# Stick-breaking attention beside a short convolution: units head by head, loads a head ahead, transposes before scores

## The chip, the cores and the metric

The kernel runs on one core of a Trainium2 chip. The metric is the device time of one execution in microseconds (us). Engines: TensorE (PE; its weight loads PEld), VectorE (DVE), ScalarE (ACT), GpSimd (POOL) and SyncE (SP), which issues the DMAs.

## The reference

One decoder layer on x of 2048 tokens by 1024, in float32. h = RMSNorm(x); one projection gives q, k, v (8 heads of 64) and B, C, u (512 columns each). q and k are normed per head. Then, side by side:

- stick-breaking attention, strictly causal: with z = q.k / 8, A[t,s] = sigmoid(z[t,s]) times the product over s < j < t of (1 - sigmoid(z[t,j])), out = A v;
- a gated convolution: y = B * conv3(C * u), causal, width 3, per channel.

Both are put side by side, multiplied by w_out and added to x; then RMSNorm and a SwiGLU FFN of width 2816, added to x.

## The kernel before, in words

Stages follow each other with all engines in step between them: qkv_stage (norm, q, k, v, written to DRAM), attend_conv_stage (the change is in it alone), and for each half of the tokens mix_stage and ffn_stage. Operands of matmuls are split into a high and a low part (fp32r), so most products are three matmuls (matmul3, L70 to L72).

attend_conv_stage goes over four **pairs** of heads. For a pair, and a head h, the 2048 queries are 8 groups g of 256 (two tiles t of 128). The keys up to a tile are cut into **units** of at most 8 blocks of 128 keys, from the last keys to the first: tiles 0 to 7 have one unit of t + 1 blocks, tiles 8 to 15 one of t - 7 blocks and one of 8. That is 24 units a head and 48 a pair, with 272 blocks. Before the change groups rise and the two heads take turns, group by group.

A unit n passes through the engines so:

- TensorE, scores(n): two matmuls of up to 512 columns per bank (L881, L882) and, on the diagonal, a mask (L885) into z, which has two banks' pairs: scores(n) wait until scan n-2 is done;
- ScalarE, sigmoids(n): sigmoid(z) to a (L675) and sigmoid(-z) back into z (L677);
- VectorE, running_product(n): a scan over the unit (L760) into stick;
- GpSimd, a_unit(n): a times stick (L821);
- TensorE, transposes(n) (L897), LAG = 3 slots later: four blocks make a **fill** of tr, which has two fills; a fill waits until VectorE is done with the fill two before it;
- ScalarE copies a fill to aT_hi (L688), VectorE subtracts it to aT_lo (L772);
- TensorE, a_times_v(gi) once all units of a group are through (L912), then o_low (ScalarE, L695) and o_sb (VectorE, L781), and a store.

Every engine runs a list of **slots**, one for each unit, in program order. In slot n VectorE does scan(n), then aT_lo(n-3); ScalarE does sigmoids(n), then aT_hi(n-3); TensorE does scores(n), half of the slot's projection steps, transposes(n-3), the other half, and at a group's end a_times_v.

Between them TensorE computes the projection of B, C and u for 512 tokens a pair: 12 outputs (NPROJ) of 8 steps of 3 matmuls into one bank, proj. A planner (own, weight, ratio) spreads the 96 steps over the slots by the columns that a slot has of its own. Before the change ScalarE copies C out of proj (L719), VectorE multiplies u (L787) and B (L799) straight from proj, GpSimd convolves (L837 to L842). ScalarE and GpSimd split the weights (w_split, L711 and L847).

SyncE issues the loads. At the start of a pair it issues q, w, k, all 8 parts of hT and v; k and v of a pair can go only when the units that read the old ones are through.

## Time and profile before

| | |
|---|---|
| median of 3 runs | 2892.89 us (2890.64 to 5896.87) |
| profiled execution | 2895.9 us, its span 2894.1 us |
| TensorE busy | 2675.9 us, 92% of the span |
| VectorE busy | 1447.6 us, 50% |
| ScalarE busy | 907.9 us, 31% |
| GpSimd busy | 557.3 us, 19% |
| DMA | 246.33 MB, mean 85 GB/s |
| mean granted TensorE clock | 0.967 of 2.4 GHz |

Times are from the start of the span. An instruction's line is that of the kernel; L70 to L72 are the helper for three matmuls. Matmuls are pipelined: one shown with 0.39 us is followed by the next after 0.23 us, so a busy TensorE is not one at its peak, and spacing is read from starts. The attention stage takes some 850 us of the span, the FFN most of the rest.

### The profile page before, as it was taken

Reading aid. Unit: us, or ns where it says so; the run is one execution under the profiler, and the core shown is the slowest. Engines: PE = TensorE matmul, PEld = TensorE weight load, DVE = VectorE, ACT = ScalarE, POOL = GpSimd, SP = SyncE. Lnnn points to the kernel's source line nnn. Section 1 sums busy time; section 2 is a strip of 40 time slices with the busy share of each in tenths; the row PEclk is TensorE's granted clock in tenths of the full one; section 3 lists DMA queues with packets and bytes.
Section 4 is the critical chain, followed back from the end, with each engine's and each line's share of the span. In section 5 each row is a group of like instructions: output and inputs, shape, how many; then the busy total and the mean of one; then the engine's idle time right before and its main releaser. Section 6 shows DMA issues by size and latency. Waiting matters only on the chain. (4 is left out here: it accounts for less than half of the span.)

```text
span 2894.1 us, 36348 instructions
## 1 busy us (share of the span) xinstructions
PE 2675.9 (92%) x12800; PEld 2205.3 (76%) x12800; DVE 1447.6 (50%) x1536; ACT 907.9 (31%) x1423; POOL 557.3 (19%) x426
## 2 busy tenths in 40 slices
PE   6999679799898898799999999999789999999998
PEld 5888567677677677587888888887678888888887
DVE  4333256566576577443454444444434444544444
ACT  3222256566566566322111111111221111111110
POOL 1222146556466466100000000000000000000000
PEclk9999889899899999899999999999899999999999
DMA  5555652531631630412111111100621111111101
GB/s 173 176 172 169 173 150 60 137 109 52 167 85 54 173 84 25 154 50 88 44 56 45 43 51 43 58 29 8 225 73 59 44 51 43 55 47 43 51 29 58
DMA packets 301153, 246.33 MB, mean 85 GB/s; under 512 B 14193, under 2 KB 272241, under 8 KB 300273
## 3 DMA queue, kind: packets, MB, share of 16 engines
q1 hardware_dynamic: 301040, 244.90, 28.3%
q8 instruction: 63, 1.03, 0.1%
q14 instruction: 50, 0.40, 0.1%
HBM read 186.13 MB, written 58.72 MB: 85 GB/s over the span
## 5 line engine op out<-in xcount | busy, mean ns | idle before, releaser
L1281 DVE TENSOR_TENSOR all_acc<-all_acc,ffn_down 128x1024 f32<-128x1024 f32 x352 | 426.0, 1220 | 374.3 <-PE ffn_down L72 356.9
L760 DVE TENSOR_TENSOR_SCAN att_stick<-att_z,att_stick 128x128 f32<-128x128 f32 (+3 forms) x192 | 331.0, 1724 | 269.5 <-ACT att_z L677 268.4
L821 POOL TENSOR_TENSOR att_a<-att_a,att_stick 128x128 f32<-128x128 f32 (+3 forms) x192 | 281.6, 1471 | 338.1 <-DVE att_stick L760 324.6
L70 PE MATMUL ffn_gate<-all_h2T_hi,ffn_gu_hi 128*128 128x512 f32 x704 | 276.6, 393 | 8.2 <-DVE ffn_gu_lo L1271 8.2
L70 PE MATMUL ffn_down<-ffn_d_hi,ffn_hid_hi 128*128 128x512 f32 x704 | 277.0, 393 | 6.2 <-DVE ffn_hid_lo L1303 6.1
L71 PE MATMUL ffn_down<-ffn_d_lo,ffn_hid_hi 128*128 128x512 f32 x704 | 276.1, 392 | 0.0
L71 PE MATMUL ffn_gate<-all_h2T_lo,ffn_gu_hi 128*128 128x512 f32 x704 | 276.0, 392 | 0.0
L72 PE MATMUL ffn_down<-ffn_d_hi,ffn_hid_lo 128*128 128x512 f32 x704 | 276.0, 392 | 0.0
L72 PE MATMUL ffn_gate<-all_h2T_hi,ffn_gu_lo 128*128 128x512 f32 x704 | 275.8, 392 | 0.0
L70 PE MATMUL ffn_up<-all_h2T_hi,ffn_gu_hi 128*128 128x512 f32 x704 | 273.9, 389 | 0.0
L71 PE MATMUL ffn_up<-all_h2T_lo,ffn_gu_hi 128*128 128x512 f32 x704 | 273.9, 389 | 0.0
L72 PE MATMUL ffn_up<-all_h2T_hi,ffn_gu_lo 128*128 128x512 f32 x704 | 273.9, 389 | 0.0
L1292 DVE TENSOR_TENSOR ffn_hid<-ffn_silu,ffn_up 128x512 f32<-128x512 f32 x88 | 60.6, 688 | 400.4 <-PE ffn_up L72 400.4
L1261 ACT ACTIVATE ffn_hid_hi<-ffn_hid 128x512 fp32r<-128x512 f32 x88 | 55.7, 632 | 605.8 <-DVE ffn_hid L1292 605.8
L897 PE MATMUL att_tr<-all_ident,att_a 128*128 128x128 f32 x1088 | 170.9, 289 | 74.6 <-DVE att_aT_lo L772 74.3
L1252 ACT ACTIVATE ffn_silu<-ffn_gate 128x512 f32<-128x512 f32 x88 | 52.7, 598 | 582.0 <-PE ffn_gate L72 582.0
L675 ACT ACTIVATE att_a<-att_z 128x128 f32<-128x128 f32 (+3 forms) x192 | 149.2, 777 | 227.1 <-PE att_z L885 157.1
L897 PEld LDWEIGHTS att_tr<-all_ident,att_a 128*128 128x128 f32 x1088 | 131.0, 147 | 115.3 <-DVE att_aT_lo L772 80.6
L70 PE MATMUL att_proj<-att_hT_hi,att_w_hi 128*128 128x512 f32 x384 | 175.4, 457 | 28.8 <-DMA att_hT_lo<-hT_lo 11.6
L772 DVE TENSOR_TENSOR att_aT_lo<-att_tr,att_aT_hi 128x512 fp32r<-128x512 f32 (+2 forms) x320 | 180.4, 594 | 28.2 <-ACT att_aT_hi L688 19.0
L1042 POOL TENSOR_TENSOR mix_msq<-mix_ss,all_eps 128x1 f32<-128x1 f32 x16 | 3.0, 190 | 965.4 <-ACT mix_square L1075 965.4
L688 ACT ACTIVATE att_aT_hi<-att_tr 128x512 fp32r<-128x512 f32 (+2 forms) x320 | 159.2, 531 | 71.6 <-PE att_tr L897 70.9
(108 smaller groups left out, 5222.2 us busy)
## 6 DMA issues: line engine op xcount, KB each, us to landing
att_w_stage<-in_w_in SPq DMA_DIRECT2D x48, 512.0 KB, 4.4
ffn_d_stage<-in_w_down SPq DMA_DIRECT2D x44, 512.0 KB, 3.4
all_stage<-in_w_gate SPq DMA_DIRECT2D x22, 512.0 KB, 3.8
all_stage<-in_w_up SPq DMA_DIRECT2D x22, 512.0 KB, 4.7
ffn_gu_stage<-in_w_gate SPq DMA_DIRECT2D x22, 512.0 KB, 3.7
ffn_gu_stage<-in_w_up SPq DMA_DIRECT2D x22, 512.0 KB, 4.7
qkv_x_t<-in_x SPq DMA_DIRECT2D x16, 512.0 KB, 4.5
hT_hi<-qkv_hT_hi SPq DMA_DIRECT2D x16, 512.0 KB, 5.4
```

Of the source, the lines that this page charges most:

```text
L70: nc.tensor.matmul(out, lhs_hi, rhs_hi, start=first, stop=False)
L71: nc.tensor.matmul(out, lhs_hi, rhs_lo, start=False, stop=False)
L72: return nc.tensor.matmul(out, lhs_lo, rhs_hi, start=False, stop=last)
L675: nc.scalar.activation(a[:, n % 4, 0:nb * P], z[:, n % 2, 0:nb * P], ACT.Sigmoid, scale=SCALE).then_inc(chance_done, 1)
L688: nc.scalar.activation(aT_hi[:, gi % 2, j0 + j:j0 + j + nj, (t % GT) * P:(t % GT + 1) * P], tr[:, f % 2, 0:nj, :], ACT.Copy).then_inc(aT_h ...
L760: nc.vector.tensor_tensor_scan(stick[:, row % 2, c0:c1][:, ::-1], z[:, n % 2, 0:nb * P][:, ::-1], stick[:, row % 2, S:S + 1].to_broadcast( ...
L772: nc.vector.tensor_tensor(aT_lo[:, gi % 2, blocks, toks], tr[:, f % 2, 0:nj, :], aT_hi[:, gi % 2, blocks, toks].bitcast(F32), ALU.subtract ...
L821: nc.gpsimd.tensor_tensor(a[:, n % 4, 0:nb * P], a[:, n % 4, 0:nb * P], stick[:, row_of[n] % 2, c0:c0 + nb * P], ALU.mult).then_inc(a_done, 1)
L897: last = nc.tensor.transpose(tr[:, f % 2, i, :], a[:, n % 4, (j + i) * P:(j + i + 1) * P], cst["ident"][:, :])
L1261: nc.scalar.activation(hid_hi[:, b, n * BANK:(n + 1) * BANK], hid[:, n % 2, :], ACT.Copy).then_inc(hid_hi_done, 1)
L1281: nc.vector.tensor_tensor(acc[:, t, :], acc[:, t, :], down[:, t % 2, :, :].rearrange("p h n -> p (h n)"), ALU.add).then_inc(acc_done, 1)
L1292: nc.vector.tensor_tensor(hid[:, n % 2, :], silu[:, n % 2, :], up[:, n % 2, :], ALU.mult).then_inc(hid_done, 1)
```

## The change

Four things:

1. **Order of units.** All groups of head 0, then all of head 1; in a head the groups go 4, 3, 5, 2, 6, 1, 7, 0.
2. **Loads.** q lies in a ring of four groups and is loaded two groups ahead, k and v a head ahead, hT and the first weights of a pair at the end of the pair before.
3. **The projection's results** are all copied out of proj by ScalarE (take), GpSimd multiplies C*u and B*conv. TensorE waits for one semaphore, proj_out.
4. **TensorE's slot**: transposes(n-3), then scores(n), then all projection steps, then a_times_v. The planner's costs are new.

VectorE's list keeps scan(n) ahead of aT_lo(n-3), ScalarE's keeps sigmoids(n) ahead of aT_hi(n-3). The first and the last pair are written out, the two between are a loop. The diff, cut:

```diff
@@ -441,7 +434,9 @@
     KB = S // P
     GW = 2 * P
     GT = GW // P
-    NG = 2 * (S // GW)
+    HG = S // GW
+    NG = 2 * HG
+    QB = 4
     SLOT = 2 * BANK
     SB = SLOT // P
     LAG = 3
@@ -451,30 +446,34 @@
     NPROJ = 3 * CT
     HALO = TAPS - 1
     COL0 = w_in.shape[1] - 3 * CD
-    assert S // BANK == PAIRS
-
-
-    units, opens = [], []
-    for gi in range(NG):
+    assert S // BANK == PAIRS and NG % QB == 0
+
+    rising = [g for g in range(HG // 2, HG)]
+    falling = [HG - 1 - g for g in rising]
+    groups = [(h, g) for h in range(2) for pair in zip(rising, falling) for g in pair]
+    units, opens, row_of, row_end = [], [], [], []
+    for gi, (h, g) in enumerate(groups):
         for i in range(GT):
-            t = GT * (gi // 2) + i
+            t = GT * g + i
             for j0 in reversed(range(0, t + 1, SB)):
                 opens.append(not units or units[-1][0] != gi)
-                units.append((gi, gi % 2, t, j0, min(SB, t + 1 - j0)))
-    NU = len(units)
+                units.append((gi, h, t, j0, min(SB, t + 1 - j0)))
+                row_of.append(len(row_end))
+            row_end.append(len(units))
+    NU, ROWS = len(units), len(row_end)
     fills = [0]
     for u in units:
         fills.append(fills[-1] + -(-u[4] // 4))
     FILLS = fills[-1]
-    assert NU % 4 == 0 and FILLS % 2 == 0
+    assert NU % 4 == 0 and FILLS % 2 == 0 and ROWS % 2 == 0
     group_units = [sum(u[0] < gi for u in units) for gi in range(NG + 1)]
-    head_end = [max(n for n, u in enumerate(units) if u[1] == h) + 1 for h in range(2)]
-
-
+    head_end = [group_units[HG], NU]
 
     FIRST, LAST = 1, NU - 1
-    own = [u[4] + (GT * (units[n - LAG][0] // 2 + 1) if n > LAG and opens[n - LAG] else 0)
-           for n, u in enumerate(units)]
+    own = []
+    for n, u in enumerate(units):
+        av = 2.1 * (groups[units[n - LAG - 1][0]][1] + 1) if opens[n - LAG] else 0
+        own.append(0.5 * u[4] + 0.45 * units[n - LAG][4] + av)
     weight = [u[4] + 1.7 for u in units]
     ratio = (sum(own[FIRST:LAST]) + 3 * NPROJ * KT) / sum(weight[FIRST:LAST])
     steps, placed, goal, spent = [[] for _ in units], 0, 0.0, 0.0
@@ -491,16 +489,13 @@
     starts = {n: k for n in range(NU) for k, i in steps[n] if i == 0}
     ends = {n: k for n in range(NU) for k, i in steps[n] if i == KT - 1}
     assert len(starts) == len(ends) == NPROJ
-
-
-    row_of, row_end = [], []
-    for n, (gi, h, t, j0, nb) in enumerate(units):
-        if j0 + nb == t + 1:
-            row_end.append(n)
-        row_of.append(len(row_end) - 1)
-        row_end[-1] = n + 1
-    ROWS = len(row_end)
-    assert ROWS % 2 == 0
+    emptied = {n + 1: k for n, k in ends.items()}
+    taken = {k: n for n, k in emptied.items()}
+    multiplied = {taken[3 * c + 1]: c for c in range(CT)}
+    tapped_at = {taken[3 * c + 1] + 1 + d: (c, d) for c in range(CT) for d in range(2)}
@@ -547,38 +549,40 @@
         tr_full, aT_hi_done, aT_lo_done = m.sem("tr_full"), m.sem("aT_hi_done"), m.sem("aT_lo_done")
         o_full, o_low_done, o_done = m.sem("o_full"), m.sem("o_low_done"), m.sem("o_done")
         o_stored = [m.sem("o_stored0"), m.sem("o_stored1")]
-        w_hi_done, w_lo_done, proj_full = m.sem("w_hi_done"), m.sem("w_lo_done"), m.sem("proj_full")
-        c_done, cu_done, conv_chain, conv_done, y_done, y_stored = (
-            m.sem(n) for n in ("c_done", "cu_done", "conv_chain", "conv_done", "y_done", "y_stored"))
+        w_hi_done, w_lo_done, proj_full, proj_out = (
+            m.sem(n) for n in ("w_hi_done", "w_lo_done", "proj_full", "proj_out"))
+        cu_done, conv_chain, conv_done, y_done, y_stored = (
+            m.sem(n) for n in ("cu_done", "conv_chain", "conv_done", "y_done", "y_stored"))
         block = m.block()
 
         def pairs(eng, body):
             body(0)
-            with eng.Fori(1, PAIRS) as p:
+            with eng.Fori(1, PAIRS - 1) as p:
                 body(p)
...
-            def load_k(p, h, keys, loaded):
-                wait(sp, z_full, NU * p + head_end[h] - NU)
+            def load_k(p, h):
+                wait(sp, z_full, NU * (p - 1) + head_end[h])
                 rows = bass.ds((2 * p + h) * HD + AD, HD)
                 for half, src in enumerate((qk_hi_dram, qk_lo_dram)):
-                    sp.dma_start(k_st[half * HD:(half + 1) * HD, h, keys].bitcast(F32),
-                                 src[rows, keys]).then_inc(loaded, DMA)
+                    sp.dma_start(k_st[half * HD:(half + 1) * HD, h, :].bitcast(F32),
+                                 src[rows, :]).then_inc(k_in[h], DMA)
 
             def load_q(p, gi):
-                h, g = gi % 2, gi // 2
-                q, gq = at(p, gi - 4, NG)
+                h, g = groups[gi]
+                q, gq = at(p, gi - QB, NG)
                 wait(sp, z_full, q * NU + group_units[gq + 1])
-                rows = bass.ds((2 * p + h) * HD, HD)
+                rows = bass.ds((2 * p + h) * HD, HD) if g else bass.ds(p * P + h * HD, HD)
                 for half in range(2):
                     part = slice(half * HD, (half + 1) * HD)
                     for dst, src in ((q_hh, qk_hi_dram), (q_ll, qk_lo_dram)):
-                        sp.dma_start(dst[part, h, g % 2, :].bitcast(F32),
-                                     src[rows, g * GW:(g + 1) * GW]).then_inc(q_in[h][g % 2], DMA)
+                        sp.dma_start(dst[part, gi % QB, :].bitcast(F32),
+                                     src[rows, g * GW:(g + 1) * GW]).then_inc(q_in[gi % QB], DMA)
 
             def load_v(p, h):
-                wait(sp, o_full, NG * p + h - 1)
+                wait(sp, o_full, NG * (p - 1) + HG * (h + 1))
                 sp.dma_start(v_st[:, h, :, :].bitcast(F32), v_dram.rearrange("(j p) h d -> p j h d", p=P)
                              [:, :, bass.ds(2 * p + h, 1), :].rearrange("p j h d -> p j (h d)")).then_inc(v_in[h], DMA)
 
...
+            def start_up():
+                load_k(0, 0)
+                load_q(0, 0)
+                load_w(0, 0)
+                for i in range(KT // 2):
+                    load_hT(0, i)
+                load_w(0, 1)
+                load_q(0, 1)
+                for i in range(KT // 2, KT):
+                    load_hT(0, i)
+                load_v(0, 0)
+                with nc.allow_non_contiguous_dma(reason="conv weights, once"):
+                    for c in range(CT):
+                        sp.dma_start(taps[:, c, :], conv_w[:, c * P:(c + 1) * P].rearrange("w p -> p w")
+                                     ).then_inc(taps_in, DMA)
+
+            def body(p):
+                if is_first(p):
+                    start_up()
+                for n, (gi, h, t, j0, nb) in enumerate(units):
+                    if opens[n]:
+                        if gi + 2 < NG:
+                            load_q(p, gi + 2)
+                        elif not is_last(p):
+                            load_q(p + 1, gi + 2 - NG)
+                        if gi >= 3 or not is_first(p):
+                            store_o(p, gi - 3)
+                    if n == 2:
+                        load_k(p, 1)
+                        if not is_first(p):
+                            store_y(p - 1, CT - 1)
+                    if n == LAG + 3:
+                        load_v(p, 1)
+                    if n in starts and starts[n] + 2 < NPROJ:
+                        load_w(p, starts[n] + 2)
+                    if n - 2 in gated and gated[n - 2] < CT - 1:
+                        store_y(p, gated[n - 2])
+                    if not is_last(p):
+                        if n == head_end[0] + 2:
+                            load_k(p + 1, 0)
+                        if n == head_end[0] + LAG + 3:
+                            load_v(p + 1, 0)
+                        for i in reloads.get(n, ()):
+                            load_hT(p + 1, i)
+                        if n == taken[NPROJ - 1]:
+                            load_w(p + 1, 0)
+                            load_w(p + 1, 1)
 
...
-                wait(act, halo_moved, 2 * (CT * p + c))
-                if isinstance(p, int) and c == 0:
-                    act.wait_ge(edges_set, 2)
-                nc.scalar.activation(cu[:, 0:HALO], halo[:, c, :], ACT.Copy).then_inc(halo_moved, 1)
-
-            def keep_halo(p, c):
-                act.wait_ge(cu_done, CT * p + c + 1)
-                nc.scalar.activation(halo[:, c, :], cu[:, BANK:BANK + HALO], ACT.Copy).then_inc(halo_moved, 1)
+            def take(p, k):
+                c = k // 3
+                if k % 3 == 1:
+                    wait(act, conv_done, CT * p + c)
+                    wait(act, halo_moved, 2 * (CT * p + c))
+                    if is_first(p) and c == 0:
+                        act.wait_ge(edges_set, 2)
+                    nc.scalar.activation(cu[:, 0:HALO], halo[:, c, :], ACT.Copy).then_inc(halo_moved, 1)
+                act.wait_ge(proj_full, NPROJ * p + k + 1)
+                if k % 3 == 0:
+                    wait(act, cu_done, CT * p + c)
+                    nc.scalar.activation(c_sb[:, :], proj[:, :], ACT.Copy).then_inc(proj_out, 1)
+                elif k % 3 == 1:
+                    nc.scalar.activation(cu[:, HALO:HALO + BANK], proj[:, :], ACT.Copy).then_inc(proj_out, 1)
+                else:
+                    wait(act, y_stored, DMA * (CT * p + c))
+                    nc.scalar.activation(y[:, :], proj[:, :], ACT.Copy).then_inc(proj_out, 1)
+                    act.wait_ge(cu_done, CT * p + c + 1)
+                    nc.scalar.activation(halo[:, c, :], cu[:, BANK:BANK + HALO], ACT.Copy).then_inc(halo_moved, 1)
 
             def w_split(p, k):
                 act.wait_ge(w_in_sem[k % 2], (DMA * NPROJ // 2) * p + DMA * (k // 2 + 1))
...
             def body(p):
+                if is_first(p):
+                    w_split(p, 0)
                 for n in range(NU):
-                    if ends.get(n - 1, 1) % 3 == 0:
-                        c = ends[n - 1] // 3
-                        act.wait_ge(proj_full, NPROJ * p + ends[n - 1] + 1)
-                        wait(act, cu_done, CT * p + c)
-                        nc.scalar.activation(c_sb[:, :], proj[:, :], ACT.Copy).then_inc(c_done, 1)
-                        set_halo(p, c)
+                    if n in emptied:
+                        take(p, emptied[n])
+                    q, b = at(p, n - LAG - 1)
+                    if opens[b] and (n - LAG - 1 > 0 or not is_first(p)):
+                        o_part(q, units[b][0] - 1)
                     sigmoids(p, n)
-                    if ends.get(n - 1, 0) % 3 == 1:
-                        keep_halo(p, ends[n - 1] // 3)
-                    if n >= LAG or not isinstance(p, int):
+                    if n >= LAG or not is_first(p):
                         aT_part(p, n - LAG)
-
-                    q, b = at(p, n - LAG - 1)
-                    if opens[b] and (n - LAG - 1 > 0 or not isinstance(p, int)):
-                        o_part(q, units[b][0] - 1)
-                    if n == 0:
-                        w_split(p, 0)
                     if n in starts and starts[n] + 1 < NPROJ:
                         w_split(p, starts[n] + 1)
+                    if n == taken[NPROJ - 1] and not is_last(p):
+                        w_split(p + 1, 0)
 
@@ -821,6 +816,11 @@
                 nc.gpsimd.tensor_tensor(a[:, n % 4, 0:nb * P], a[:, n % 4, 0:nb * P],
                                         stick[:, row_of[n] % 2, c0:c0 + nb * P], ALU.mult).then_inc(a_done, 1)
 
+            def c_times_u(p, c):
+                pool.wait_ge(proj_out, NPROJ * p + 3 * c + 2)
+                nc.gpsimd.tensor_tensor(cu[:, HALO:HALO + BANK], cu[:, HALO:HALO + BANK], c_sb[:, :],
+                                        ALU.mult).then_inc(cu_done, 1)
+
             CHAIN = 2 * TAPS - 2
 
             def convolve(p, c, part):
@@ -842,22 +842,33 @@
                 nc.gpsimd.tensor_tensor(conv[:, :], conv[:, :], tapped[:, :],
                                         ALU.add).then_inc(conv_done if part == TAPS - 1 else conv_chain, 1)
 
+            def gate(p, c):
+                pool.wait_ge(proj_out, NPROJ * p + 3 * c + 3)
+                pool.wait_ge(conv_done, CT * p + c + 1)
+                nc.gpsimd.tensor_tensor(y[:, :], y[:, :], conv[:, :], ALU.mult).then_inc(y_done, 1)
+
...
+                    w_split(p, 0)
                 for n in range(NU):
-                    for part in range(TAPS):
-                        k = ends.get(n - 1 - part, 0)
-                        if k % 3 == 1:
-                            convolve(p, k // 3, part)
+                    if n in multiplied:
+                        c_times_u(p, multiplied[n])
+                    if n in tapped_at:
+                        c, d = tapped_at[n]
+                        for part in ((0, 1), (2,))[d]:
+                            convolve(p, c, part)
+                    if n in gated:
+                        gate(p, gated[n])
                     a_unit(p, n)
-                    if n == 0:
-                        w_split(p, 0)
                     if n in starts and starts[n] + 1 < NPROJ:
                         w_split(p, starts[n] + 1)
+                    if n == taken[NPROJ - 1] and not is_last(p):
+                        w_split(p + 1, 0)
 
             pairs(pool, body)
 
...
-                        wait(pe, y_done, CT * p + k // 3)
-                    elif k % 3 == 1:
-                        pe.wait_ge(c_done, CT * p + k // 3 + 1)
-                    else:
-                        pe.wait_ge(cu_done, CT * p + k // 3 + 1)
+                    wait(pe, proj_out, NPROJ * p + k)
                 last = matmul3(nc, proj[:, :], w_hi[:, k % 2, i, :], w_lo[:, k % 2, i, :],
                                hT_hi[:, i, :], hT_lo[:, i, :], i == 0, i == KT - 1)
                 if i == KT - 1:
@@ -935,17 +937,13 @@
 
             def body(p):
                 for n in range(NU):
+                    if n >= LAG or not is_first(p):
+                        transposes(p, n - LAG)
                     scores(p, n)
-
-                    early = 0 if n in starts else (len(steps[n]) + 1) // 2
-                    for k, i in steps[n][:early]:
-                        project_step(p, k, i)
-                    if n >= LAG or not isinstance(p, int):
-                        transposes(p, n - LAG)
-                    for k, i in steps[n][early:]:
+                    for k, i in steps[n]:
                         project_step(p, k, i)
                     q, b = at(p, n - LAG)
-                    if opens[b] and (n > LAG or not isinstance(p, int)):
+                    if opens[b] and (n > LAG or not is_first(p)):
                         a_times_v(q, units[b][0] - 1)
 
             pairs(pe, body)
...
```

## Rows read from the trace of the kernel before

**Rows 1.** The attention stage by pair: stretch and length in us, busy us (instructions) by engine.

```profile
342.60:561.00 218.40, 176.38 (x984) 144.44 (x985) 125.69 (x142) 122.88 (x208) 118.34 (x79) 0.91 0.45 118
561.00:768.20 207.20, 180.21 (x1043) 148.69 (x1042) 136.48 (x155) 126.88 (x216) 121.81 (x81) 0.95 0.40 109
...
971.70:1164.50 192.80, 171.82 (x997) 142.17 (x998) 127.13 (x146) 124.08 (x212) 114.27 (x76) 0.97 0.27 72
```

**Rows 2.** TensorE in order of time: start us, us, then the merged instructions.

```profile
376.20 0.39 PE L70 MATMUL att_proj<-att_hT_hi,att_w_hi 128*128 128x512 f32 x1
376.42 0.39 PE L71 MATMUL att_proj<-att_hT_lo,att_w_hi 128*128 128x512 f32 x1
...
558.38 0.28 PE L912 MATMUL att_o<-att_aT_lo,att_v_st 128*128 128x256 f32 x1
558.50 0.28 PE L912 MATMUL att_o<-att_aT_hi,att_v_st 128*128 128x256 f32 x1
...
706.70 0.82 PE L897 MATMUL att_tr<-all_ident,att_a 128*128 128x128 f32 x6
```

**Rows 3.** Waits in the whole kernel, and what the projection's engines waited for.

```profile
PE att_tr L897 <- DVE att_aT_lo L772: 74.3, 69, 4.3
...
  DMA att_hT_lo<-hT_lo: 29.1, 7
...
  DMA att_w_stage<-in_w_in: 18.9, 3
```

**Rows 4.** An 8-block unit from its scores to the next transposes, all engines.

```profile
705.08 0.39 PE L881 MATMUL att_z<-att_k_st,att_q_hh 128*128 128x512 f32 x1
...
706.20 1.03 ACT L675 ACTIVATE att_a<-att_z 128x1024 f32<-128x1024 f32 x1 [0.57 <-PE att_z L882]
...
707.13 1.02 ACT L677 ACTIVATE att_z<-att_z 128x1024 f32<-128x1024 f32 x1
...
708.18 2.35 DVE L760 TENSOR_TENSOR_SCAN att_stick<-att_z,att_stick 128x1024 f32<-128x1024 f32 x1 [1.27 <-ACT att_z L677]
...
710.45 0.99 DVE L772 TENSOR_TENSOR att_aT_lo<-att_tr,att_aT_hi 128x512 fp32r<-128x512 f32 x2
...
711.17 1.16 PE L897 MATMUL att_tr<-all_ident,att_a 128*128 128x128 f32 x8 [2.18 <-DVE att_aT_lo L772]
```

**Rows 5.** A 5-block unit, all engines.

```profile
701.57 0.44 PE L881 MATMUL att_z<-att_k_st,att_q_hh 128*128 128x512 f32 x1
...
703.86 1.55 DVE L760 TENSOR_TENSOR_SCAN att_stick<-att_z,att_stick 128x640 f32<-128x640 f32 x1 [0.27 <-ACT att_z L677]
...
705.33 1.26 DVE L772 TENSOR_TENSOR att_aT_lo<-att_tr,att_aT_hi 128x512 fp32r<-128x512 f32 x2
```

**Rows 6.** Granted clock (PEclk) of three stretches, and eight transposes at either level.

```profile
566.00:576.00 10.00, 6.72 (x20) 5.01 (x21) 3.32 (x6) 4.14 (x9) 5.27 (x3) 0.50 0.88 197
870.00:890.00 20.00, 18.49 (x119) 15.70 (x118) 12.92 (x13) 13.88 (x22) 9.96 (x6) 1.00 0.31 83
1173.00:1182.00 9.00, 5.82 (x24) 4.55 (x24) 5.31 (x10) 3.96 (x7) 2.00 (x1) 0.50 0.03 7
...
563.88 1.12 PE L897 MATMUL att_tr<-all_ident,att_a 128*128 128x128 f32 x8 [2.43 <-DVE att_aT_lo L772]
...
566.04 1.97 PE L897 MATMUL att_tr<-all_ident,att_a 128*128 128x128 f32 x8 [0.73 <-DVE att_aT_lo L772]
```

**Rows 7.** Reads of proj and what follows: count, busy us, mean ns, idle before.

```profile
L842 POOL TENSOR_TENSOR att_conv<-att_conv,att_tapped 128x512 f32<-128x512 f32 x32 | 41.1, 1285 | 2.5
...
L799 DVE TENSOR_TENSOR att_y<-att_proj,att_conv 128x512 f32<-128x512 f32 x16 | 11.0, 686 | 14.8 <-POOL att_conv L842 11.3 <-issue 3.4
...
L719 ACT ACTIVATE att_c_sb<-att_proj 128x512 f32<-128x512 f32 x16 | 9.6, 599 | 2.7 <-PE att_proj L72 2.6
```

**Rows 8.** The busiest stretch of the DMA engines at a joint.

```profile
550.00:570.00 20.00, 14.60 (x92) 12.26 (x92) 11.95 (x15) 11.23 (x19) 13.19 (x10) 0.88 0.98 272
```

**Rows 9.** The last instruction of the stage on VectorE.

```profile
1188.58 0.42 DVE L781 TENSOR_TENSOR att_o_sb<-att_o,att_o_low 64x256 f32<-64x256 f32 x1 [6.36 <-ACT att_o_low L695]
```

More of the change, by code:

```diff
@@ L493, in attend_conv_stage @@
     assert len(starts) == len(ends) == NPROJ
-    row_of, row_end = [], []
-    for n, (gi, h, t, j0, nb) in enumerate(units):
-        if j0 + nb == t + 1:
-            row_end.append(n)
-        row_of.append(len(row_end) - 1)
-        row_end[-1] = n + 1
-    ROWS = len(row_end)
-    assert ROWS % 2 == 0
+    emptied = {n + 1: k for n, k in ends.items()}
+    taken = {k: n for n, k in emptied.items()}
+    multiplied = {taken[3 * c + 1]: c for c in range(CT)}
+    tapped_at = {taken[3 * c + 1] + 1 + d: (c, d) for c in range(CT) for d in range(2)}
+    gated = {taken[3 * c + 2]: c for c in range(CT)}
+    assert all(taken[3 * c + 2] >= taken[3 * c + 1] + 2 for c in range(CT)) and max(taken.values()) < NU
+    reloads = {n + 1: [i for k, i in steps[n] if k == NPROJ - 1] for n in range(NU)}
     def key_slot(n):
@@ L512, in at, with is_first, is_last @@
         return (p, n) if n >= 0 else (p - 1, n + per)
+    def is_first(p):
+        return isinstance(p, int) and p == 0
+    def is_last(p):
+        return isinstance(p, int) and p == PAIRS - 1
     with ExitStack() as stack:
@@ L537, in attend_conv_stage @@
         proj = m.ps("proj", [P, BANK])
-        k_first = [m.sem("k_first0"), m.sem("k_first1")]
         k_in, v_in = [m.sem("k_in0"), m.sem("k_in1")], [m.sem("v_in0"), m.sem("v_in1")]
-        q_in = [[m.sem(f"q_in{h}{b}") for b in range(2)] for h in range(2)]
+        q_in = [m.sem(f"q_in{b}") for b in range(QB)]
         hT_in = [m.sem(f"hT_in{i}") for i in range(KT)]
@@ L602, in store_o @@
                 p, gi = at(p, gi, NG)
[L603 removed]
+                h, g = groups[gi]
                 sp.wait_ge(o_done, NG * p + gi + 1)
[L605 removed]
+                rows = bass.ds((2 * p + h) * HD, HD) if g else bass.ds(2 * (p * HD) + h * HD, HD)
+                sp.dma_start(mixT_dram[rows, g * GW:(g + 1) * GW],
                              o_sb[:, gi % 2, :]).then_inc(o_stored[gi % 2], DMA)
[L608 to L653 removed]
@@ L753, in running_product @@
                 if j0 + nb == t + 1:
-                    if row >= 2 or not isinstance(p, int):
+                    if row >= 2 or not is_first(p):
                         q, r = at(p, row - 2, ROWS)
@@ L781, in o_part @@
                 nc.vector.tensor_tensor(o_sb[:, gi % 2, :], o[0:HD, 0:GW], o_low[:, :], ALU.add).then_inc(o_done, 1)
-            def c_times_u(p, c):
-                dve.wait_ge(halo_moved, 2 * (CT * p + c) + 1)
-                dve.wait_ge(c_done, CT * p + c + 1)
-                dve.wait_ge(proj_full, NPROJ * p + 3 * c + 2)
-                nc.vector.tensor_tensor(cu[:, HALO:HALO + BANK], proj[:, :], c_sb[:, :], ALU.mult).then_inc(cu_done, 1)
             def body(p):
                 for n in range(NU):
-                    k = ends.get(n - 1, 0)
-                    if k % 3 == 1:
-                        c_times_u(p, k // 3)
-                    if k % 3 == 2:
-                        c = k // 3
-                        dve.wait_ge(proj_full, NPROJ * p + k + 1)
-                        dve.wait_ge(conv_done, CT * p + c + 1)
-                        wait(dve, y_stored, DMA * CT * p + DMA * c)
-                        nc.vector.tensor_tensor(y[:, :], proj[:, :], conv[:, :], ALU.mult).then_inc(y_done, 1)
                     running_product(p, n)
-                    if n >= LAG or not isinstance(p, int):
+                    if n >= LAG or not is_first(p):
                         aT_part(p, n - LAG)
                     q, b = at(p, n - LAG - 1)
-                    if opens[b] and (n - LAG - 1 > 0 or not isinstance(p, int)):
+                    if opens[b] and (n - LAG - 1 > 0 or not is_first(p)):
                         o_part(q, units[b][0] - 1)
@@ L830, in convolve @@
                 if part == 0:
-                    if isinstance(p, int) and c == 0:
+                    if is_first(p) and c == 0:
                         pool.wait_ge(taps_in, DMA * CT)
@@ L867, in scores @@
                 gi, h, t, j0, nb = units[n]
[L868 removed]
                 if opens[n]:
[L870 to L872 removed]
+                    if gi % HG == 0:
                         pe.wait_ge(k_in[h], 2 * DMA * p + 2 * DMA)
[L874 removed]
+                    pe.wait_ge(q_in[gi % QB], 4 * DMA * (NG // QB) * p + 4 * DMA * (gi // QB + 1))
                 wait(pe, scan_done, NU * p + n - 1)
@@ L880, in scores @@
                     out, keys = z[:, n % 2, b0:b1], slice(j0 * P + b0, j0 * P + b1)
-                    nc.tensor.matmul(out, q_hh[:, h, g % 2, tile], k_st[:, h, keys], start=True, stop=False)
-                    last = nc.tensor.matmul(out, q_ll[:, h, g % 2, tile], k_st[:, h, keys],
+                    nc.tensor.matmul(out, q_hh[:, gi % QB, tile], k_st[:, h, keys], start=True, stop=False)
+                    last = nc.tensor.matmul(out, q_ll[:, gi % QB, tile], k_st[:, h, keys],
                                             start=False, stop=not diagonal)
```

67 lines of the change are left out of this document (6 added, 61 removed).

## The prediction

> **What bounds the kernel now.** Everything that the change touches lies in the attention stage, whose four head pairs begin at 342.6, 561.0, 768.2 and 971.7 us; the last result of the stage is written at 1189.0 [rows 1, 9]. TensorE is busy for 0.81 to 0.89 of each pair, VectorE for 0.58 to 0.66, ScalarE and GpSimd for less, so TensorE's own work comes first. How much of it is work and not pipelining: a 512-column matmul follows the last one after 0.23 us at full clock, a 256-column one after 0.12 us (0.117 as the mean of a long run of them), and six transposes take 0.82 us with a tail of some 0.2 us, so 0.105 to 0.11 us each [rows 2]. A pair has 96 projection steps of 3 matmuls (288 x 0.23 = 66 us), 272 key blocks of scores (each 2 x 0.057 = 31 us) and 32 masks (3 us), 272 transposes (29 us) and 288 products with v (32 us): 161 us. A pair takes 193 to 218 us. The rest is in the waits: ahead of the transposes TensorE waits 74.3 us in all for VectorE's aT_lo, the one large wait it has; and at the joints of the pairs it waits for loads (29.1 us for hT; ScalarE 18.9 us for w) [rows 3]. So TensorE comes close to being the bound, because its waits are short, and they are short for a reason that the change takes away.
>
> **The reason.** VectorE's list for slot n is scan(n), then aT_lo(n-3). The transposes of slot n need the tr banks that aT_lo(n-4) frees, and that stands behind scan(n-1). Today scores(n) come ahead of this wait: they need only scan(n-2). So the loop from scores to scores over TensorE, ScalarE and VectorE closes once in **two** slots. The trace shows it: the scan that starts at 703.86 runs to 705.41, and the next unit's scores start at 705.08, before its end [rows 4, 5].
>
> **Part 1, the order inside a slot: the loop closes in one slot.** After the change scores(n+1) stand behind the transposes of unit n-2, these behind aT_lo(n-3), this behind scan(n), this behind both sigmoids of n, and these behind scores(n). Nothing in the chain can start early; z's two banks no longer help. Its price is in the trace. For a unit of 8 blocks [rows 4]: scores start 705.08, first sigmoid 706.20 (a), second 707.13 (z), scan 708.18, aT_lo 710.45, next transposes 711.17: 6.09 us. For one of 5 blocks [rows 5]: scores 701.57, scan 703.86, aT_lo 705.33, and with 0.67 us for it and 0.05 to the next engine 706.05: 4.48 us. From both: 1.79 us + 0.537 us per block.
> The new order of a pair has 48 units and 272 blocks. The wait is there where unit n-2 or n-3 has over 4 blocks (two fills of tr). That fails six times a pair (slots 1, 2, 19, 25, 26, 43, 36 blocks together), where TensorE's own work decides: I count 20 us for the six. The other 42 slots have 236 blocks: 42 x 1.79 + 236 x 0.537 = 202 us. To it comes what stands between the wait and the scores: the transposes of the last fill, 130 in the 42 slots x 0.11 = 14 us; and where both units have two fills (22 slots), the second aT_lo, some 0.45 us = 10 us. Sum 202 + 14 + 10 + 20 = **246 us a pair**, against 193 to 218. TensorE's 161 us fit under it: projection and products with v come behind the scores and run while the chain is on the other engines; only the six free slots are counted by TensorE's work.
> Bounds: below, the hops could be shorter (both samples are ones in which each link started when the one before ended), 5% or 12 us a pair less; above, ScalarE's added work may get into the chain (part 3), 5% more.
>
> **Part 2, TensorE's clock.** In the new order TensorE works 161 of 246 us, with a lull in nearly every slot: in 21 of 48 slots the chain is 2.0 to 3.4 us longer than the work. In the dense stretch at 870 us the granted clock is 1.00 (the 2.4 GHz level), at 566 to 576 us, behind waits of 2.43 us and 0.73 us, it is 0.50 (1.2 GHz), and in 1173 to 1182 us, the stage's drain, where TensorE does nothing but 24 transposes with waits between, also 0.50 [rows 6]. At the low level the same eight transposes take 1.97 instead of 1.12 us [rows 6], and the scores double too (0.93 us more for 8 blocks). Work at the low level fills the lulls, so after a slot or so the clock comes back, as it did in that joint. I count ten to twelve falls a pair at about 1 us each: 12 us a pair. Bounds: 0; and at most the low clock for half of the time, 24 us for scores, masks and last transposes (31 + 3 + 14 = 48 at full clock), with the lost cover some 35 us.
> The Trainium skill (TensorE: Matmul & The Clock Gate, Part 4, PE-mode transpose) says that transposes don't count as work for the clock. By that rule the lulls would be wider, and the term nearer to 35 us a pair (+140 us in all). The sum goes by the 12 us above, since the rows don't tell transposes from idling.
>
> **Part 3, what moves to ScalarE and GpSimd.** The c, C*u and y reads of proj go to ScalarE (32 more copies of 0.60 us = 19 us in the stage), the two products to GpSimd (32 of 1.3 us at most = 41 us), 32 of 0.69 us leave VectorE (22 us) [rows 7]. ScalarE does its copies before sigmoids(n), while TensorE stands at the transposes; GpSimd works 114 to 122 us of a pair [rows 1] and has three slots for each a. I count nothing. Cover gone, it is 19 us at most.
>
> **Part 4, the loads.** k, v and q come a head ahead, so the joints' waits end. One new wait: ScalarE's w_split for the next pair stands behind unit 46, its w load behind 4 MB of hT that are issued from slot 44 on. The DMAs moved 272 GB/s at their best [rows 8], so 4.5 MB need 17 us, and from the start of slot 44 to that place are 16 us less some 2 us until the first load. I count 4 us, three times: 12 us; behind that ScalarE wait stand sigmoids(47), and all of the chain. Bounds 0 and 10 us each. At the start the first scores need a whole k (1 MB) and not a quarter: 2 us; then hT as before, some 5 us of waiting beside a chain of 8-block units.
>
> **Part 5, the ends.** The drain from the last scores (about 1164.5, where the fourth stretch of [rows 1] is cut) to 1189.0 [rows 9] is three 8-block units and 32 products; now the last units have 1 and 2 blocks: 3 us.
>
> **The sum.** Start 345 + 5, four pairs 984, clock 48, w 12, drain 3: the stage ends at 1397 against 1189, **+208 us**. The profiled execution took 2895.9 us (span 2894.1), 3 us over the median of the runs shown: 2896 + 208 = 3104.
>
> **The rivals.**
> - *Balance wins (faster).* If the transposes don't wait for scan(n), because aT_lo is ahead often enough, the gain is the joints: a pair falls to TensorE's 161 us plus its dense stretches' slack (0.92 busy at 870 us [rows 6]), 175 us; 4 x 175 + 353 = 1053, so 136 us less: 2760 us. It decides if aT_lo(n-3) could go before scan(n); the listing of VectorE has it behind. Chance 0.03.
> - *The waits cancel.* If only half of the slots are gated (say, where fills are shared in another way than I read), a pair takes 205 us and the time stays: 2890 us. Chance 0.03.
> - *The clock stays low.* If the lulls keep the clock at 0.50 for the whole stage, TensorE's 161 us become 322 and the bound, 350 + 4 x 322 + 10 = 1648: +459, 3355 us. For it speaks the drain, which stayed at 0.50; against it, that at the low level TensorE is busy without lulls, and behind such work the clock came back at the joint. Chance 0.05. The Trainium skill (the same page, "HAM oscillation") describes kernels whose every burst starts slow after a wait; by that rule this case is the one to expect.
>
> **How the numbers follow.** The forecast has 0.89: slower by about 7%. Low end: chain 5% shorter (-49), no fall of the clock (-48), no wait for w (-12): 2995; not all at once, 3020. High end: chain 5% longer, clock at its upper bound for part (+60): 3210. What a measurement of this kernel can't tell from no change is about 2%, 58 us: all of the forecast's range is past it. Faster 0.03, same 0.03, slower 0.94.
>
> **What would show it.** The wait of TensorE's transposes for aT_lo grows from 74 us to some 300 us; scores start right behind the transposes, and scan(n) starts 3.1 us behind the scores of an 8-block unit in every slot; scan starts of neighbouring 8-block slots 6 to 7 us apart; pairs of 246 to 270 us, all four nearly alike; granted clock between 0.75 and 0.95 in the stage; the FFN as before. Wrong it would be if VectorE showed aT_lo(n-3) done while scan(n) still ran, if pairs took under 215 us, or if ScalarE's copies stood between transposes and sigmoids.

## The result, and the profile after

The changed kernel takes 3148.19 us (median of 4 runs, 3140.77 to 3156.74) against 2892.22: ratio 1.089, 95% interval 1.085 to 1.092. It is slower by 256 us, where 208 was forecast. Its profiled execution took 3156.74 us, its span is 3155.0 us.

The page: busy us by engine, then TensorE's busy tenths and its granted clock in 40 slices. TensorE's share falls from 92% to 87%, and the slices of the attention stage (the 5th to the 18th) show it at 5 to 7 tenths and at 0.7 to 0.9 of the clock, without the peaks and dips of before.

```profile
PE 2753.5 (87%) x12800; PEld 2261.8 (72%) x12800; DVE 1430.5 (45%) x1504; ACT 913.3 (29%) x1455; POOL 595.4 (19%) x458
...
PE   6999577677767767776899999999978999999999
...
PEclk9999788898988989988999999999989999999999
```

The four pairs of the changed kernel, from first scores to first scores (the fourth to its last scores), columns as in [rows 1]: 266 to 282 us each against 193 to 218, granted clock 0.84 to 0.90 against 0.91 to 0.97. VectorE is 17 us less busy in the whole kernel than before (1430.5 against 1447.6) and ScalarE 5 us more (913.3 against 907.9), so neither accounts for the time.

```profile
344.20:626.30 282.10, 203.12 (x1002) 164.88 (x1002) 126.50 (x138) 128.34 (x220) 132.22 (x89) 0.84 0.36 98
626.30:896.30 270.00, 198.48 (x1043) 161.89 (x1041) 129.16 (x144) 128.37 (x224) 130.11 (x88) 0.87 0.29 78
896.30:1168.60 272.30, 196.60 (x1043) 160.94 (x1041) 129.06 (x144) 128.25 (x224) 129.95 (x88) 0.88 0.29 78
1168.60:1434.40 265.80, 195.30 (x1031) 159.44 (x1030) 127.03 (x141) 125.66 (x219) 126.97 (x86) 0.90 0.18 47
```

Behind the stage the time is the same: from its last VectorE instruction to the end of the span are 1705 us in both kernels (3155.0 - 1450.0, and 2894.1 - 1189.0). So all of the time is in the attention stage.

The waits of its engines: us in total, number of waits, the longest. TensorE's transposes wait 294.2 us for aT_lo, against 74.3 [rows 3], and VectorE's scan 582 us for the sigmoids.

```profile
DVE att_stick L770 <- ACT att_z L683: 582.2, 190, 12.4
...
PE att_tr L905 <- DVE att_aT_lo L782: 294.2, 151, 8.7
...
ACT att_w_hi L726 <- DMA att_w_stage<-in_w_in: 47.1, 6, 16.1
```

One 8-block slot of the changed kernel, from its scores to the next (slot 45 of the second pair), answers to [rows 4]. Read it downwards: each row starts when the one above ends, or within 0.1 us of it (the transposes when the first of the two aT_lo is through), and the scores at 881.75 come right behind the transposes. Of what the next scores need, only ScalarE's copy to aT_hi, which isn't among the rows, runs beside another link, the scan. 7.05 us for one unit. Before, the scores at 705.08 started while the scan of the unit ahead still ran [rows 4, 5].

```profile
874.70 0.48 PE L889 MATMUL att_z<-att_k_st,att_q_hh 128*128 128x512 f32 x1
...
875.91 1.03 ACT L681 ACTIVATE att_a<-att_z 128x1024 f32<-128x1024 f32 x1 [4.02 <-PE att_z L890]
...
876.84 1.02 ACT L683 ACTIVATE att_z<-att_z 128x1024 f32<-128x1024 f32 x1
...
877.89 2.35 DVE L770 TENSOR_TENSOR_SCAN att_stick<-att_z,att_stick 128x1024 f32<-128x1024 f32 x1 [3.22 <-ACT att_z L683]
...
880.16 1.13 DVE L782 TENSOR_TENSOR att_aT_lo<-att_tr,att_aT_hi 128x512 fp32r<-128x512 f32 x2
...
880.88 1.12 PE L905 MATMUL att_tr<-all_ident,att_a 128*128 128x128 f32 x8 [2.05 <-DVE att_aT_lo L782]
...
881.75 0.31 PE L889 MATMUL att_z<-att_k_st,att_q_hh 128*128 128x128 f32 x1
```

And the joint between the second and the third pair on ScalarE: it stands at the weights for 7.75 us, and sigmoids of slot 47 (892.59) behind it.

```profile
882.80 1.07 ACT L694 ACTIVATE att_aT_hi<-att_tr 128x512 fp32r<-128x512 f32 x2
891.63 1.06 ACT L726 ACTIVATE att_w_hi<-att_w_stage 128x1024 fp32r<-128x1024 f32 x1 [7.75 <-DMA att_w_stage<-in_w_in]
892.59 0.37 ACT L681 ACTIVATE att_a<-att_z 128x256 f32<-128x256 f32 x1
```

### The profile page after: what moved, and what is told of

It is laid out like the page before. It is cut to its first block and busy times, and to the rows that moved or that the text cites. A ratio compares the mean times of both kernels' runs of the same rounds, so it can differ in the third digit from the quotient of the medians.

```text
span 3155.0 us, 35761 instructions
## 1 busy us (share of the span) xinstructions
PE 2753.5 (87%) x12800; PEld 2261.8 (72%) x12800; DVE 1430.5 (45%) x1504; ACT 913.3 (29%) x1455; POOL 595.4 (19%) x458
## 5 line engine op out<-in xcount | busy, mean ns | idle before, releaser
L770 DVE TENSOR_TENSOR_SCAN att_stick<-att_z,att_stick 128x128 f32<-128x128 f32 (+5 forms) x192 | 331.5, 1727 | 588.2 <-ACT att_z L683 582.2
L905 PE MATMUL att_tr<-all_ident,att_a 128*128 128x128 f32 x1088 | 193.9, 316 | 296.3 <-DVE att_aT_lo L782 294.2
L905 PEld LDWEIGHTS att_tr<-all_ident,att_a 128*128 128x128 f32 x1088 | 138.5, 158 | 353.0 <-DVE att_aT_lo L782 198.2
L816 POOL TENSOR_TENSOR att_a<-att_a,att_stick 128x128 f32<-128x128 f32 (+5 forms) x192 | 282.3, 1471 | 535.2 <-DVE att_stick L770 535.1
L681 ACT ACTIVATE att_a<-att_z 128x128 f32<-128x128 f32 (+5 forms) x192 | 149.1, 777 | 500.5 <-PE att_z L893 344.1
L889 PE MATMUL att_z<-att_k_st,att_q_hh 128*128 128x512 f32 (+2 forms) x320 | 150.6, 470 | 18.8 <-DMA att_q_ll<-qk_lo 15.4
```

The lines of the kernel that those rows point to most:

```text
L681: nc.scalar.activation(a[:, n % 4, 0:nb * P], z[:, n % 2, 0:nb * P], ACT.Sigmoid, scale=SCALE).then_inc(chance_done, 1)
L770: nc.vector.tensor_tensor_scan(stick[:, row % 2, c0:c1][:, ::-1], z[:, n % 2, 0:nb * P][:, ::-1], stick[:, row % 2, S:S + 1].to_broadcast( ...
L816: nc.gpsimd.tensor_tensor(a[:, n % 4, 0:nb * P], a[:, n % 4, 0:nb * P], stick[:, row_of[n] % 2, c0:c0 + nb * P], ALU.mult).then_inc(a_done, 1)
L889: nc.tensor.matmul(out, q_hh[:, gi % QB, tile], k_st[:, h, keys], start=True, stop=False)
L905: last = nc.tensor.transpose(tr[:, f % 2, i, :], a[:, n % 4, (j + i) * P:(j + i + 1) * P], cst["ident"][:, :])
```

## The experiments

Eleven kernels, in three sets; every ratio is to the kernel before on the same chip. A difference in us between two runs can cross chips; the kernel before took 2890.96 to 2892.22 us on all of them.

**1. e_swap: scores first again, the rest of the rewrite kept.**

```
-transposes(p, n - LAG); scores(p, n)
+scores(p, n); transposes(p, n - LAG)
```

> The changed kernel with one thing undone: in TensorE's slot the scores of n come ahead of the transposes of n-3 again; the projection steps stay behind both. Theory (the loop scores, sigmoids, scan, aT_lo, transposes closes in one slot): with scores first it closes in two slots, TensorE's own 161 us a pair and its waits decide again, a pair takes 190 to 210 us, the kernel 2830 to 2900 us. Rival (the other parts of the rewrite cost the time: unit order, copies on ScalarE, loads): pairs stay near 270 us, the kernel above 3080 us.

Measured: 2879.71 us, ratio 0.997 (0.995 to 0.998). Pairs of 201 to 210 us (the third is below), the wait for aT_lo in the whole kernel 113.0 us, longest 13.1.

```profile
756.90:958.00 201.10, 175.22 (x1039) 147.20 (x1040) 128.53 (x144) 130.69 (x224) 129.75 (x88) 0.96 0.37 97
```

```profile
PE att_tr L905 <- DVE att_aT_lo L782: 113.0, 88, 13.1
```

One pair of lines swapped on one engine is worth 268 us. The rest of the rewrite costs nothing and gains 12 us as it stands.

**2. e_half: TensorE's list of before.**

```
-transposes; scores; all steps
+scores; half of the steps; transposes; the other half
```

> The changed kernel with TensorE's list of before: scores, half of the projection steps, transposes, the other half. Theory: as with scores first alone, and the wait for aT_lo is covered by projection steps, so 5 to 20 us a pair less than it: pairs of 180 to 195 us, the kernel 2780 to 2860 us. Rival (the rest of the rewrite costs the time): above 3080 us.

Measured: 2869.27 us, ratio 0.992 (0.991 to 0.994). The cover by projection steps is worth 10 us, 2.6 a pair: less than expected. Pairs take 198 to 206 us, above the 180 to 195 expected; the kernel is 9 us outside the range. Run 7 shows a part of what hid the gain: the joint.

**3. e_oldtr: the old kernel with the new order of TensorE alone.**

```
-scores; half of the steps; transposes; the other half
+transposes; scores; all steps
```

> The kernel before with one part of the change alone: TensorE does the transposes, then the scores, then all projection steps. Theory: the loop closes in every slot, its sum over the same 48 units is again about 246 us a pair, to which the joints and the clock come: pairs of 255 to 280 us, the kernel 3110 to 3200 us. Rival (the order inside the slot matters little): 2880 to 2950 us.

Measured: 3159.21 us, ratio 1.093 (1.091 to 1.094). The second pair, and the wait:

```profile
641.90:908.20 266.30, 196.38 (x1043) 159.02 (x1042) 133.85 (x152) 124.93 (x216) 121.55 (x81) 0.90 0.29 80
```

```profile
PE att_tr L897 <- DVE att_aT_lo L772: 283.7, 148, 4.4
```

In another order of units, with other loads and with proj read by VectorE, the new order on TensorE costs 267 us. This is the whole effect of the change, and 11 us over. (The edit also puts all projection steps behind the scores; by runs 1 and 2 that part is worth some 10 us.) The first pair took 300.2 us, outside of the 255 to 280 expected; why wasn't looked into. The others took 264 to 270.

**4. e_aT: transposes still first, but the other two lists turned as well.**

```
 # ScalarE
-sigmoids(p, n); aT_part(p, n - LAG)
+aT_part(p, n - LAG); sigmoids(p, n)
 # VectorE
-running_product(p, n); aT_part(p, n - LAG)
+aT_part(p, n - LAG); running_product(p, n)
```

> The changed kernel, TensorE's list as changed (transposes first), but ScalarE does aT_hi of n-3 ahead of the sigmoids of n and VectorE aT_lo of n-3 ahead of scan n. Theory: then the transposes of the next slot need an aT_lo that stands ahead of scan n and not behind it; the loop opens to two slots though TensorE's order is untouched, and the kernel takes 2800 to 2920 us. Rival (transposes ahead of scores cost by themselves, by delaying the scores on TensorE): near 3150 us.

Measured: 2840.18 us, ratio 0.983 (0.981 to 0.985). TensorE's list is that of the change, transposes ahead of scores, and the wait for aT_lo is down to 66.1 us:

```profile
PE att_tr L905 <- DVE att_aT_lo L782: 66.1, 28, 13.3
```

So it is not the transposes' own time ahead of the scores that costs. What costs is that aT_lo stands behind a scan that stands behind the scores. The rival falls. ScalarE's and VectorE's lists were turned together in every run that has this edit; what either does alone wasn't run.

**5. e_wload: the next pair's weights ahead of its hT.**

```
-load_hT(p + 1, i) ...; load_w(p + 1, 0); load_w(p + 1, 1)
+load_w(p + 1, 0); load_w(p + 1, 1); load_hT(p + 1, i) ...
```

> The changed kernel, the two weight loads of the next pair issued ahead of the next pair's hT loads and not behind them. Theory: ScalarE's wait for w at the three joints (7.75 us at one of them) goes, the last slot of a pair takes 4.5 instead of 10.1 to 11.2 us: 15 to 30 us less, 3120 to 3135 us. Rival (the wait is hidden, or hT comes later by as much and TensorE's first projection steps wait): 3140 to 3155 us.

Measured: 3128.11 us, ratio 1.083 (1.080 to 1.086), 20 us less than the changed kernel. ScalarE's waits for w go from 47.1 us in 6 waits to the three in the first 34 us of the stage:

```profile
ACT att_w_hi L726 <- DMA att_w_stage<-in_w_in: 24.8, 3, 16.2
```

**6 and 7. The same edit on top of runs 4 and 2 (e_aT_w, e_half_w).**

> The changed kernel with both: aT_hi ahead of the sigmoids on ScalarE, aT_lo ahead of the scan on VectorE, and the weights ahead of hT at the joint. Theory: the two waits are separate, the last slot of a pair (15.1 us with the first edit alone) falls to about 4, so 25 to 35 us less than with the first edit alone: 2805 to 2820 us. Rival (the wait at the joint turns into one for hT or for another engine): 2830 to 2845 us.

> The changed kernel with TensorE's list of before (scores, half of the steps, transposes, the other half) and the weights ahead of hT at the joint. Theory: 25 to 35 us less than without the second edit (2869 us): 2834 to 2846 us; so the rewrite without its TensorE order is faster than the kernel before once the joint is repaired. Rival (the wait turns into one for hT): 2860 to 2872 us.

Measured: 2796.94 us, ratio 0.967 (0.965 to 0.968), 8 us below the range, and 2834.15 us, ratio 0.979 (0.977 to 0.981), at its lower end. The same wait is worth 43 and 35 us here, more than in the slow kernel: the faster the slots before the joint, the longer ScalarE stands at the same DMA. In e_aT it was 11.7 to 12.6 us at the three joints; at the second:

```profile
737.48 1.06 ACT L726 ACTIVATE att_w_hi<-att_w_stage 128x1024 fp32r<-128x1024 f32 x1 [12.26 <-DMA att_w_stage<-in_w_in]
```

Why the loop is open in e_aT_w is to be seen in its slots 33 to 35, all engines: the scores at 661.76 start 0.53 us before the scan at 659.94 ends (662.29); the transposes at 664.00 come behind that scan and the aT_lo of 662.23, but the scores of 661.76 didn't need either. Two units are in flight, as in the kernel before.

```profile
659.94 2.35 DVE L770 TENSOR_TENSOR_SCAN att_stick<-att_z,att_stick 128x1024 f32<-128x1024 f32 x1 [0.99 <-ACT att_z L683]
...
660.94 1.06 PE L905 MATMUL att_tr<-all_ident,att_a 128*128 128x128 f32 x8
...
661.60 1.09 ACT L694 ACTIVATE att_aT_hi<-att_tr 128x512 fp32r<-128x512 f32 x2
...
661.76 0.48 PE L889 MATMUL att_z<-att_k_st,att_q_hh 128*128 128x512 f32 x1
...
662.23 1.29 DVE L782 TENSOR_TENSOR att_aT_lo<-att_tr,att_aT_hi 128x512 fp32r<-128x512 f32 x2
...
664.00 0.60 PE L905 MATMUL att_tr<-all_ident,att_a 128*128 128x128 f32 x4
664.08 1.55 DVE L770 TENSOR_TENSOR_SCAN att_stick<-att_z,att_stick 128x640 f32<-128x640 f32 x1 [0.56 <-ACT att_z L683]
...
664.35 0.47 PE L889 MATMUL att_z<-att_k_st,att_q_hh 128*128 128x512 f32 x1
```

**8. e_fill: TensorE's lulls filled.** Behind a slot's own work in 28 of 48 slots (the expectation says 33, a miscount) 6 to 27 small matmuls, whose results are not used.

```
+for _ in range(fillers[n]):
+    nc.tensor.matmul(o[:, GW:GW + P], ident_bf, ident_bf, start=True, stop=True)
```

> The changed kernel with idle work in TensorE's lulls: in 33 of 48 slots 6 to 27 matmuls of 128 bf16 columns (identity by identity) into the unused half of the bank of the products with v, about 0.06 us each at full clock, placed behind the slot's own work; the result is not used. It probes the term for the clock. Theory: the lulls are what lets the granted clock fall, its cost is 12 to 25 us a pair in the changed kernel (pairs of 267 to 282 us against a chain of 246); filled lulls keep the clock at 1.00 in most slots, pairs take 250 to 262 us and the kernel 3070 to 3125 us, faster by 25 to 80 us than the changed kernel though it does more. Rival (the surplus over 246 us is in other waits, the clock plays no part): 3150 us or more, by the fillers that get in the way.

Measured: 3120.8 us, ratio 1.079 (1.078 to 1.081), 27 us less than the changed kernel, though TensorE does 457 more matmuls a pair. Its second and fourth pair:

```profile
617.10:877.60 260.50, 209.87 (x1499) 174.55 (x1498) 129.19 (x144) 128.42 (x224) 129.93 (x88) 0.95 0.31 82
...
1145.30:1399.60 254.30, 205.82 (x1467) 172.22 (x1466) 127.04 (x141) 125.67 (x219) 126.78 (x86) 0.96 0.20 50
```

The granted clock rises from 0.87 and 0.90 to 0.95 and 0.96, and these pairs fall from 270.0 and 265.8 to 260.5 and 254.3 us. The first and the third gain less: 273.4 us at 0.91 and 267.7 at 0.93, against 282.1 and 272.3, both outside of the 250 to 262 expected.

**9. e_fill_w: runs 5 and 8 together.**

> The changed kernel with both the fillers in TensorE's lulls and the next pair's weights ahead of hT. Theory: clock (3148 to 3121 alone) and joint (3148 to 3128 alone) are separate terms and add: 27 + 20 us, 3095 to 3108 us; what is left over the chain of 246 us a pair is 3 to 12 us a pair. Rival (they overlap: the clock's falls come from the wait at the joint): 3115 to 3121 us.

Measured: 3098.12 us, ratio 1.071 (1.069 to 1.074), 50 us less than the changed kernel: 27 + 20 were expected, so the two terms add up. The third pair:

```profile
862.90:1117.90 255.00, 211.24 (x1499) 175.44 (x1498) 129.18 (x144) 128.28 (x224) 129.87 (x88) 0.95 0.30 81
```

**10. e_aT_sw: run 6 with scores first.** Transposes and scores swapped back in e_aT_w.

> The fastest so far (aT_hi and aT_lo of n-3 ahead, weights ahead of hT: 2797 us), with the scores ahead of the transposes on TensorE. Theory: once aT_lo is ahead of the scan, TensorE's order no longer closes the loop either way; now aT_hi, and behind it the sigmoids, wait for transposes that stand behind scores (1 us for 8 blocks), so it is the same or up to 40 us slower: 2790 to 2840 us. Rival (scores first is always better): under 2785 us.

Measured: 2787.39 us, ratio 0.964 (0.962 to 0.967): the lowest of all. It misses both forecasts by under 3 us, the 2790 to 2840 of the theory and the rival's less than 2785, so it decides for neither. It is 10 us under run 6, but the intervals of the two ratios overlap. Pairs take 175 to 186 us, the last at the full clock, and the transposes wait 9.5 us for aT_lo, against 26.2 in run 6; their wait for a is as there (17.7 and 18.4):

```profile
345.80:531.80 186.00, 168.52 (x993) 142.01 (x994) 125.92 (x135) 126.33 (x217) 126.69 (x85) 0.95 0.49 136
...
894.40:1069.60 175.20, 166.86 (x1032) 141.94 (x1030) 128.89 (x142) 126.27 (x223) 127.98 (x88) 1.00 0.33 85
```

```profile
PE att_tr L905 <- POOL att_a L816: 17.7, 8, 2.3
...
PE att_tr L905 <- DVE att_aT_lo L782: 9.5, 5, 6.3
```

**11. e_old_aT: the old kernel with transposes first and both other lists turned.**

> The kernel before with transposes first on TensorE (3159 us alone) and aT_hi ahead of the sigmoids, aT_lo ahead of the scan; unit order, loads and reads of proj as before. Theory: the loop opens as it did in the changed kernel (3148 to 2840): 2830 to 2900 us, so the order of the three lists, not the rewrite around it, makes or breaks the time. Rival (it needs the new unit order): above 3000 us.

Measured: 2883.21 us, ratio 0.997 (0.996 to 0.998). 276 us come back, as in run 4 (308). The new unit order isn't needed for that; the rest of the rewrite makes 2883 into 2840, and with the loads mended 2797.

## Why the prediction was right, and what was off

- **The loop closes in one slot (part 1): right, and shown.** The order of transposes and scores on TensorE makes the time in both kernels (runs 1 and 3), and it goes again without touching them when aT_lo comes ahead of the scan (runs 4 and 11). The wait for aT_lo was forecast at some 300 us and is 294.2; scan behind scores at 3.1 us, measured 3.19 (877.89 - 874.70).
- **246 us a pair: right as a floor.** In run 9, where the joint is mended and the clock in part, each of the 48 slots occurs up to four times; the sum of the fastest of each is 246.6 us. No whole pair is as short: they take 255 to 262. By the prediction's own rule (1.79 + 0.537 a block, 0.11 a transpose of the last fill, 0.45 for a second aT_lo) an 8-block slot behind units of two fills takes 6.98 and measured 7.04, slot 12 takes 5.04 and measured 5.19; the six free slots take 20.7 for 20. Two kinds are off and partly cancel: slot 3, behind a 1-block unit whose aT_lo is short, 6.18 for 6.53, and slot 5, with six projection steps, 7.91 for 6.53. In the changed kernel slots 7, 9 and 15 of the second pair are 0.8 to 0.9 us longer than the fastest of run 9.
- **The clock (part 2): right in kind, short in size.** Forecast 12 us a pair. The second pair took 270.0; less 246 and the joint's 7 leaves 17 us. The trace's record of the granted clock has 12 falls to 0.50 in that pair, as many as forecast, so the price of one, about 1 us, was too low: some 1.4 us, if all of the 17 is the clock's. Run 8 took 27 us off by filling part of the lulls, which shows the term for that much; that the rest of the 17 is the clock too is an inference from the granted clock alone. The Trainium skill's rule on transposes (TensorE: Matmul & The Clock Gate, Part 4) was priced at 35 in the prediction: the trace is nearer to the sum's 12. Why the clock falls where it does wasn't tried.
- **The joint (part 4): right in kind, too small.** 20 us (run 5) for 12. ScalarE was at the place earlier than the 4.5 MB, and waited 7.3, 7.75 and 8.4 us at the three joints and not 4.
- **ScalarE's and GpSimd's added work (part 3): nothing, as counted.** e_swap, which has all of it, is no slower than the kernel before, and with the loop closed the kernel that has it takes 3148 us and the one without it 3159 (run 3). The work alone was never taken out, so a few us either way stay open.
- **The drain and the first pair (part 5): too small.** From the last scores to the stage's end are 15.7 us (1450.0 - 1434.3), of which 3.6 are slot 47: 12 us for 3. The first pair is 12 us longer than the second, for 5. Together 16 us.
- **The sum.** 54 us are missing between first scores and the stage's end (1106 against 1052): clock 4 x 5 = 20 (if each pair lost what the second did), drain 9, joint 8, first pair 7, fourth pair 6, third pair 3. The two written-out pairs' 7 and 6 are about what their slower slots make (last section).
- **The joints before: misread, without weight in the sum.** The 29.1 us for hT and 18.9 for w [rows 3] don't lie at the joints. All of them are in the first pair, hT from 348.5 to 368.7 us, w from 344.9 to 382.1, and the 29.1 count TensorE's matmuls (11.6) and weight loads (17.5) for the same stops. Two of the six rows on w and the matmuls:

```profile
359.26 1.06 ACT L711 ACTIVATE att_w_hi<-att_w_stage 128x1024 fp32r<-128x1024 f32 x1 [12.77 <-DMA att_w_stage<-in_w_in]
...
363.66 0.80 PE L70 MATMUL att_proj<-att_hT_hi,att_w_hi 128*128 128x512 f32 x1 [5.21 <-DMA att_hT_lo<-hT_lo]
```

- **The rivals.** The clock's staying low for the whole stage didn't come: 0.84 to 0.90. *The waits cancel* would have left pairs of 205 us; they take 266 to 282. *Balance wins* needed aT_lo ahead of the scan, which VectorE's list excluded; runs 4, 6 and 10 are that case, made by hand. 2760 was its time, 2787 the lowest that was reached.
- **Where the rewrite's own gain went.** e_swap gains 12 us, and the first pair alone gives more than that (200.6 us against 218.4), where TensorE's waits for hT are gone. At the joints its loads cost: ScalarE waits 11.7, 10.5 and 11.7 us for w, where the kernel before has no wait for w or hT at all. Without these waits (run 7) the rewrite is at 0.979 (0.977 to 0.981).

## What to carry to other kernels

In a pipeline over in-order engines, follow the loop from a unit's first instruction through every engine's list back to the next unit's first, and count in how many slots it closes: a swap of two independent steps on the engine that is busiest can take a second unit out of flight, and z's and tr's double buffers, which both kernels have, don't bring it back. It can be cured in either place, in TensorE's list (run 1) or in the lists that hold the freeing step back (here VectorE's and ScalarE's, run 4); both together gave 10 us more at most (run 10). A third fill of tr, which would free the transposes in another way, wasn't tried. When a bound is lifted, look again at every load that was just in time: the same DMA cost 20 us in the slow kernel and 43 in the fast one.

## What the runs showed of the hardware that was not expected

Pairs that are written out (the first and the last) pass a slot's chain more slowly than the two in the register loop, at the same clock. TensorE in slot 45 of the first pair, scores, next transposes, next scores:

```profile
604.85 0.48 PE L889 MATMUL att_z<-att_k_st,att_q_hh 128*128 128x512 f32 x1
...
611.24 1.07 PE L905 MATMUL att_tr<-all_ident,att_a 128*128 128x128 f32 x8 [2.27 <-DVE att_aT_lo L782]
612.07 0.31 PE L889 MATMUL att_z<-att_k_st,att_q_hh 128*128 128x128 f32 x1
```

6.39 us to the transposes and 7.22 to the next scores, against 6.18 and 7.05 in the second pair above; the fourth pair has 6.40 and 7.21, the third 6.16 and 7.04. The instructions last as long; three hops between engines take longer, from scores to sigmoid 0.06 us (1.27 and 1.21), from sigmoid to scan 0.08, from aT_lo to transposes 0.09. In both written-out pairs the slots whose chain decides are mostly 0.12 to 0.19 us longer, some 6 us a pair; those that TensorE's own work decides aren't (slot 25: 4.85 and 4.86). The cause wasn't tried.

TensorE gets faster by being given more: 457 useless matmuls a pair took 27 us off the kernel (run 8), by way of the granted clock.
